# Two-layer hybrid encoder step on one core: order at the ends of FFN-in, the pool windows, the gates, the row products and the sample transposes

## The reference

```python
def _swiglu(u, w_in, w_out):
    h = u @ w_in                        # 1024 -> 2 x 2816
    a, b = h[..., :D_FF], h[..., D_FF:]
    return (jax.nn.silu(a) * b) @ w_out
# layer 0's mixer: means over the last 2, 4, 8, 16 rows per group of 256 channels,
# minus the row itself, times a 256x256 matrix per group
# layer 1's mixer (mLSTM): p = u @ w_in gives q, k, v, o and 2 x 4 gates; chunked scan over
# tokens with running maxima m of the gate sums; h = num / max(|den|, exp(-m)); norm; gate by o
for i in range(DEPTH):
    x = x + 0.5 * _swiglu(_rmsnorm(x, norm_ffn1[i]), ffn1_w_in[i], ffn1_w_out[i])
    x = x + mixer_i(_rmsnorm(x, norm_mix[i]))
    x = x + 0.5 * _swiglu(_rmsnorm(x, norm_ffn2[i]), ffn2_w_in[i], ffn2_w_out[i])
return _rmsnorm(x, norm_final), states
```

## Time and profile before

| what | value |
|---|---|
| median of 3 runs | 1940.64 us (1940.33 to 1942.73) |
| profiled execution, its own time | 1941.61 us |
| its span in the trace | 1939.8 us |
| PE busy | 1889.8 us (97%) |
| DVE busy | 1265.5 us (65%) |
| ACT busy | 861.1 us (44%) |
| POOL busy | 348.7 us (18%) |
| mean granted TensorE clock | 0.989 |

### The profile page before, as it was taken

One profiled execution on the slowest core, in us unless ns is written; L12 is line 12 of the kernel. 1 busy time (PEld: TensorE's weight loads), 2 busy tenths in 40 slices (PEclk: granted clock), 3 DMA queues, 4 the chain that ended last, 5 costly groups with the idle time before them and its releaser, 6 DMA issues.

```text
span 1939.8 us, 34552 instructions
## 1 busy us (share of the span) xinstructions
PE 1889.8 (97%) x13912; PEld 1865.1 (96%) x13912; DVE 1265.5 (65%) x1999; ACT 861.1 (44%) x1503; POOL 348.7 (18%) x365
## 2 busy tenths in 40 slices
PE   7999999998999999999999999999999999999996
PEld 6999999998999999999999999999989999999996
DVE  6884487657884488678853886452546987448742
ACT  6552355346553255445532553222434465235521
POOL 2220122121220121132201221200002522012122
PEclk8999999999999999999999999999999999999998
DMA  6763577323764476438644763321113476357531
GB/s 182 163 152 104 118 168 151 104 70 71 168 147 110 117 165 143 109 93 183 135 130 106 169 135 96 93 96 56 55 44 110 103 174 156 91 131 163 124 90 64
DMA packets 115854, 234.70 MB, mean 121 GB/s; under 512 B 13233, under 2 KB 13249, under 8 KB 115697
## 3 DMA queue, kind: packets, MB, share of 16 engines
q1 hardware_dynamic: 76464, 160.59, 27.7%
q0 software_dynamic: 38208, 69.42, 21.8%
q10 hardware_dynamic: 1024, 2.49, 0.4%
HBM read 228.92 MB, written 3.53 MB: 120 GB/s over the span
## 4 chain that ended last, share of the span: by engine, by line
PE 85%; DVE 5%; DMA 4%; issue 4%; ACT 2%; POOL 0%; DVEq 0%; ACTq 0%; POOLq 0%
PE ps L1688 43%; PE ps L1678 39%; DVE w_lo L1140 2%; DMA raw_z<-in_ffn_in 1%; DMA raw_y<-in_ffn_in 1%; ACT w_hi L712 1%; DMA w_raw<-in_ffn_out 1%; PE ps L1992 0%; DMA x<-in_x 0%; PE ps L1995 0%; PE ps L1982 0%; DVE tmp L1259 0%; DMA raw_a<-in_ffn_in 0%; DVE rstd L1211 0%; DVE raw_z L1146 0%
## 5 line engine op out<-in xcount | busy, mean ns | idle before, releaser
L1688 PE MATMUL ps<-u,w_hi 128*128 128x288 f32 x4928 | 994.7, 298 | 29.7 <-DVE w_lo L1140 11.0
L1688 PEld LDWEIGHTS ps<-u,w_hi 128*128 128x128 f32 x4928 | 796.7, 189 | 36.4 <-DVE w_lo L1140 19.4
L1688 PE MATMUL ps<-u,w_lo 128*128 128x288 f32 x2464 | 731.0, 297 | 0.0
L1688 PEld LDWEIGHTS ps<-u,w_lo 128*128 128x128 f32 x2464 | 465.6, 189 | 0.0
L1678 PE MATMUL ps<-h_hi,w_lo 128*128 128x288 f32 x1408 | 302.8, 296 | 0.0
L1678 PE MATMUL ps<-h_hi,w_hi 128*128 128x288 f32 x1408 | 302.7, 296 | 0.0
L1678 PE MATMUL ps<-h_lo,w_hi 128*128 128x288 f32 x1408 | 302.5, 296 | 0.0
L712 ACT ACTIVATE w_hi<-w_raw 128x768 fp32r<-128x768 f32 (+3 forms) x164 | 137.1, 837 | 341.4 <-PE ps L1678 305.1
L1140 DVE TENSOR_TENSOR w_lo<-w_raw,w_hi 128x768 fp32r<-128x768 f32 (+3 forms) x164 | 170.4, 1039 | 175.2 <-ACT w_hi L712 172.6
L574 POOL DMA_DIRECT2D raw_y<-in_ffn_in x88 | 75.8, 864 | 864.0 <-DVE raw_z L1146 847.8
L1678 PEld LDWEIGHTS ps<-h_lo,w_hi 128*128 128x128 f32 x1408 | 226.6, 189 | 0.0
(11 more groups left out here) (246 smaller groups left out, 2179.0 us busy)
## 6 DMA issues: line engine op xcount, KB each, us to landing
raw_a<-in_ffn_in SPq DMA_DIRECT2D x132, 256.0 KB, 4.2
w_raw<-in_ffn_out SPq DMA_DIRECT2D x64, 384.0 KB, 3.1
raw_y<-in_ffn_in SPq DMA_DIRECT2D x88, 256.0 KB, 3.6
raw_x<-in_ffn_in SPq DMA_DIRECT2D x88, 256.0 KB, 2.7
raw_x<-in_ffn_in POOLq DMA_DIRECT2D x88, 256.0 KB, 6.1
raw_y<-in_ffn_in POOLq DMA_DIRECT2D x88, 256.0 KB, 5.0
raw_z<-in_ffn_in POOLq DMA_DIRECT2D x88, 256.0 KB, 4.7
w_raw<-in_ffn_out SPq DMA_DIRECT2D x64, 320.0 KB, 2.9
```

The costliest lines, as they stand in the source:

```text
L1688: mm = pe.matmul(dst, w, m, start=prod in ("M1", "M2", "M5") and kp == 0 and p == 0, stop=kp == KP - 1 and p == 2, skip_group_check=prod i ...
```

## The change

It has six parts, each with its place in the diff.

1. Ends of FFN-in, DVE. After M6(10), M2(10), M3(9), M3(10) and M4(10) DVE no longer calls `ahead`; after `h_mul(10)` it makes up for it. The splits of the first two units of FFN-out thus move behind `up_two(10)`, those of the next two behind `h_mul(10)`.
2. Ends of FFN-in, ACT. `silu(10)` goes ahead of `h_high(9)`, both go ahead of the copies that `ahead` makes at M3(10) and M4(10).
3. At the mLSTM's norm `ahead(U_M)` goes ahead of `root` on ACT and of `rstd_of` on DVE. It splits one unit, the fourth projection's weights, which take the entries of the gates' weights.
4. Gates. PE does the first two steps of the first projection between the gates' seventh and eighth step, and the norm's mean comes behind the projection's third step.
5. Row products. "cols" and "mb"(0) move from behind the first v projection to the third and the sixth step of the second one.
6. Pool windows: the 15 columns of the next chunk join the product of 128 columns (143 in one), so five products a tile in place of eight. The fp32 products for the sample (L1957, L1968, L2020) become transposes, 8, 4 and 8 of them.

```diff
@@ scalar, ffn_in
-                    ahead(u)
+                    if (prod, n) == ("M4", PAIRS - 1):
+                        silu(f, ph, PAIRS - 1)
+                        h_high(f, ph, PAIRS - 2)
+                    if (prod, n) != ("M3", PAIRS - 1):
+                        ahead(u)
...
-                h_high(f, ph, PAIRS - 2)
-                silu(f, ph, PAIRS - 1)
                 h_high(f, ph, PAIRS - 1)
@@ scalar, before the mLSTM
+            ahead(U_M)
             root(N_MIX)
             act.dma_start(c_st[1][:, :, :], a["state_c"]).then_inc(state_landed, 16)
-            ahead(U_M)
@@ vector, ffn_in
-                    ahead(u)
+                    if (prod, n) != ("M3", PAIRS - 2) and (n < PAIRS - 1 or prod in ("M1", "M5", "M7")):
+                        ahead(u)
                 h_mul(f, ph, PAIRS - 1)
+                ahead(f.unit(ph, "M4", PAIRS - 1))
                 h_low(f, ph, PAIRS - 1)
@@ tensor, pool_windows
-                    pe.matmul(ps[:, window_bank(g) + m, HIST:CH], zs[0], bands[:, g, IN + HIST:NEXT], start=True, stop=True)
+                    pe.matmul(ps[:, bank, HIST:CH + HIST], zs[0], bands[:, g, IN + HIST:START],
+                              start=False, stop=True, skip_group_check=True)
                     for c in range(1, NB - 1):
-                        pe.matmul(ps[:, window_bank(g) + m, c * CH:(c + 1) * CH], zs[c], bands[:, g, IN:NEXT],
-                                  start=True, stop=False)
-                        mm = pe.matmul(ps[:, window_bank(g) + m, c * CH:c * CH + HIST], zs[c - 1], bands[:, g, NEXT:START],
-                                       start=False, stop=True)
+                        end = min(SEQ, (c + 1) * CH + HIST)
+                        mm = pe.matmul(ps[:, bank, c * CH:end], zs[c], bands[:, g, IN:IN + end - c * CH],
+                                       start=False, stop=True, skip_group_check=True)
@@ tensor, gates and first projection
+            for k in range(DT - 1):
+                gates_mm(k)
+            pe.wait_ge(lo_split, U_M + 2)
+            for k in range(DT):
+                if k == 2:
+                    gates_mm(DT - 1).then_inc(unit_used, 1)
+                elif k == 3:
+                    norm(N_MIX)
+                mm = block_mm(U_M + 1, k, u_tile(k), 2, k == 0, k == DT - 1)
             mm.then_inc(unit_used, 1)
-            norm(N_MIX)
-            pe.wait_ge(x_ready, 5 * DT)
-            for g in range(1, 9):
+            for g in range(2, 9):
@@ tensor, items
-                    mm = pe.matmul(ps[0:DEC_SEQ, b + 1, 0:P], og[:, n, SEQ:TOK], ident[:, :],
-                                   start=True, stop=True)
+                    mm = pe.transpose(ps[0:DEC_SEQ, b + 1, 0:P], og[:, n, SEQ:TOK], ident[:, :])
@@ tensor, v projections
-                project(U_M + 9 + t, 2 * ((9 + t) % 2))
+                inside = {2: lambda: item("cols", 0, 0), 5: lambda: item("mb", 0, 1)} if t == 1 else {}
+                project(U_M + 9 + t, 2 * ((9 + t) % 2), inside)
                 for k, (kind, n) in enumerate(AFTER_V[t], ITEM_AT[t]):
-                    item(kind, n, k)
+                    if t:
+                        item(kind, n, k)
@@ tensor, heads_back
-                pe.matmul(ps[:, b + 1, 0:DEC_SEQ], v_one[0:DEC_SEQ, NB - 1, h, d0:d0 + P],
-                          ident[0:DEC_SEQ, 0:DEC_SEQ], start=True, stop=True).then_inc(y_psum, 1)
+                pe.transpose(ps[:, b + 1, 0:DEC_SEQ], v_one[0:DEC_SEQ, NB - 1, h, d0:d0 + P],
+                             ident[0:DEC_SEQ, 0:DEC_SEQ]).then_inc(y_psum, 1)
```

More of the change, by code:

```diff
@@ L1798, in u_tile, with project @@
                 return um_hi[:, k, :], um_lo[:, k, :]
-            def project(n, bank, middle=None, middle_at=3, each=None):
+            def project(n, bank, inside={}, each=None):
                 pe.wait_ge(lo_split, n + 1)
@@ L1808, in project @@
                         mm.then_inc(each, 1)
-                    if k == middle_at and middle:
-                        middle()
+                    if k in inside:
+                        inside[k]()
             def norm_cols(n):
@@ L1879, in pool_windows @@
                     zs = [z[:, g, c, m * P:(m + 1) * P] for c in range(NB - 1)]
-                    pe.matmul(ps[:, window_bank(g) + m, 0:HIST], zs[0], bands[:, g, START:LAST], start=True, stop=True)
-                    pe.matmul(ps[:, window_bank(g) + m, HIST:CH], zs[0], bands[:, g, IN + HIST:NEXT], start=True, stop=True)
+                    bank = window_bank(g) + m
+                    pe.matmul(ps[:, bank, 0:HIST], zs[0], bands[:, g, START:LAST], start=True, stop=True)
+                    pe.matmul(ps[:, bank, HIST:CH + HIST], zs[0], bands[:, g, IN + HIST:START],
+                              start=False, stop=True, skip_group_check=True)
                     for c in range(1, NB - 1):
-                        pe.matmul(ps[:, window_bank(g) + m, c * CH:(c + 1) * CH], zs[c], bands[:, g, IN:NEXT],
-                                  start=True, stop=False)
-                        mm = pe.matmul(ps[:, window_bank(g) + m, c * CH:c * CH + HIST], zs[c - 1], bands[:, g, NEXT:START],
-                                       start=False, stop=True)
+                        end = min(SEQ, (c + 1) * CH + HIST)
+                        mm = pe.matmul(ps[:, bank, c * CH:end], zs[c], bands[:, g, IN:IN + end - c * CH],
+                                       start=False, stop=True, skip_group_check=True)
                     mm.then_inc(pool_psum, 1)
@@ L1915, in _, with gates_mm @@
             pe.wait_ge(x_ready, 5 * DT - 1)
-            for k in range(DT):
+            def gates_mm(k):
                 pe.wait_ge(u_ready, DT + k + 1)
@@ L1921, in _ @@
                                        u[:, h * HALF:(h + 1) * HALF], start=k + p == 0,
-                                       stop=k + p == DT)
+                                       stop=k + p == DT, skip_group_check=True)
+                return mm
+            for k in range(DT - 1):
[7 more added lines that the diff above has]
+                mm = block_mm(U_M + 1, k, u_tile(k), 2, k == 0, k == DT - 1)
             mm.then_inc(unit_used, 1)
-            norm(N_MIX)
-            pe.wait_ge(x_ready, 5 * DT)
-            for g in range(1, 9):
+            for g in range(2, 9):
                 if g > 2:
@@ L1964, in item @@
                                   start=True, stop=True)
-                        if L == P:
-                            mm = pe.transpose(ps[:, b + 1, h * P:(h + 1) * P], k_c, ident[:, :])
-                        else:
-                            mm = pe.matmul(ps[0:L, b + 1, h * P:(h + 1) * P], k_c, ident[:, :],
-                                           start=True, stop=True)
+                        mm = pe.transpose(ps[0:L, b + 1, h * P:(h + 1) * P], k_c, ident[:, :])
                 mm.then_inc(core_psum, 1)
@@ L2031, in _ @@
                     middle, behind = IN_O[j]
-                    project(U_M + 17 + j, 2 * ((17 + j) % 2), middle=lambda: in_o(middle))
+                    project(U_M + 17 + j, 2 * ((17 + j) % 2), {3: lambda: in_o(middle)})
                     in_o(behind)
                 else:
-                    project(U_M + 17 + j, 2 * ((17 + j) % 2), middle=first_heads, middle_at=DT - 2)
+                    project(U_M + 17 + j, 2 * ((17 + j) % 2), {DT - 2: first_heads})
             pe.wait_ge(proj_read, 26)
```

## The result

The changed kernel takes 1933.34 us (median of 6 runs) where the kernel before, on the same chip, takes 1941.68 us; the ratio is 0.9942 with a 95% interval of 0.9925 to 0.9958. Two of its six executions were slow, 3057.7 us at a mean granted clock of 0.55 and 4606.3 us at 1.00, for a reason that no run here shows; the ratio leaves them out, and the median of the other four is 1931.5 us. A second measurement on another occasion gave 0.9948 (0.9928 to 0.9968). It is faster by 0.5 to 0.6%, where 0.47% was forecast, and both medians lie in the forecast range. The profiled execution took 1928.8 us with a span of 1927.0, and that of before 1941.61 with 1939.8.

The account below looks back on a forecast made before the run. PE was taken as the bound, busy 1889.8 of 1939.8 us. Terms 3.0 + 0.6 + 1.0 + 0.9 + 3.6 = 9.1 us, from the median of 1940.64, gave 1931.5 us, 0.47% faster; range 1927.0 to 1937.0.

Parts of the forecast that it names:

- Ends of FFN-in, 3.0 us: At M4(10) in four of eight stages, PE's waits of 0.33, 1.17, 0.18 and 1.35 us behind `up_two` all go.
- The step on ACT: At the ends of FFN-in, `silu(10)` ahead of `h_high(9)` on ACT only shortens `h_mul(10)`'s wait; no gain of its own.
- the slack of 0.6 us: At step 11 of FFN-out's first output tile, `h_low(10)` ends near 358.0 us and PE wants it at 358.6.
- the slower rival: DVE bounds FFN-in's end: moved splits wait for copies, `h_low(10)` 2.5 us late in eight stages; 1951 us, chance 0.05.
- Pool windows, 0.6 us: In the pool stage each tile saves 0.31 us; DVE's chain moves up by two tiles' worth; ends 0 and 2.5.
- Gates, 1.0 us: Two projection steps fill 1.6 us of the 1.68 us wait; a 0.5 us wait for DVE's read comes before the third projection.
- Row products, 0.9 us: Behind the 4-row products among the v projections, fewer clock falls; between 3.4 us won and 1.7 us lost.
- Half a fall: For the row products, taken between both 1.7 us falls to 1.2 GHz going and a third coming; 0.9 us.
- Transposes, 3.6 us: Sample's fp32 products as transposes: 0.20 us saved for each of 16, 0.1 for each of 4 in "sk".
- the lower bound: For the transposes, 1.5 us, if a pause now lies before the transpose's successor.
- The page's rule: Transposes do not count as busy for the clock gate; by it, 3.6 us less one or two falls.

Follow-up runs that it names:

- the transposes' own experiment: The kernel before with only the decode sample's fp32 products against the identity turned into transposes; ratio 0.9984 (0.9972 to 0.9997).
- The parts measured alone: The kernel before with one part each: ends of FFN-in (ratio 0.9971), pool windows (0.9987), the sample's transposes (0.9984), row products (1.0010).

## Why the prediction was right, step by step

The sum was 9.1 us; the median of 1931.5 us lies 10.2 below that of before, and the ratios give 11.3 (8.2 to 14.6) and 10.1 us. The direction and the places were right, but most terms were off, in both directions. Ends and windows were 2.0 us too low, the gates, the row products and the transposes 2.2 us too high, so that the sum fits this well is in part luck.

- **Ends of FFN-in, 3.0 us:** right for the profile it was read from, and low as a mean: the old order's pauses at M4(10) are 2.4 to 5.8 us over five executions, and with the other short pauses the ends are worth about 4.1. The step on ACT was wrong. "Only shortens `h_mul(10)`'s wait" is false: with ScalarE's old order the slack of 0.6 us is used up, and about 5 us stand at step 11. The mechanism of the slower rival was real; what kept it away is the half of the edit that I had costed at nothing. The rival asked whether the copies for the splits are late, and it is `h_high(9)` behind a copy that waits for a transfer.
- **Pool windows, 0.6 us:** the term was mis-sized, about 1.5 us by itself. I took 0.31 us for a full product and scaled it by 143/128. But 0.31 is the price of one that stands behind a product of 15 columns; behind another wide one it is 0.24, in the kernel before (431.20 to 431.44 us) as in the 143-column row after. The tile saves 0.55 us and not 0.31, twice on the path, and 0.3 us more comes from z(3).
- **Gates, 1.0 us:** 0.5. The order of copy, table load, root and read came as worked out, and PE reached the third projection within 0.2 us of where I had it, but the read of q ended 0.5 us later: the copy began 0.9 us behind the start of the gates' last step where I had 0.6, from reciprocal to read it took 9.2 us and not 9.1, and the rest is rounding. A pause of 0.5 became one of 1.14.
- **Row products, 0.9 us:** -0.3. Half a fall was a guess between two cases, and neither came: the falls stay, one to five of them, and the switches cost 0.3. What was missed is that their number changes with the execution of one and the same program.
- **Transposes, 3.6 us:** 3.1 by the ratio. The single prices were wrong in both directions: 0.43 us for each of the eight in "vt" where I took 0.20, a loss of 0.15 for each of the four in "sk" where I took a gain of 0.1, and 0.16 in `heads_back` (the step is 0.20 us, it was 0.36); a pause of 0.76 us came back at "sk"(3), the kind named for the lower bound.
- **The page's rule.** The Trainium skill, TensorE: Matmul & The Clock Gate, Part 4: PE-mode transpose, says that transposes do not count as busy for the clock gate in the way other products do; by that the clock could fall where they replace products. Among the items the measurement decides against it: 1.00 over their stretch in the transposes' own experiment and in every other profile with them. In `heads_back` it stays open, as the fall there came with and without them.

The parts measured alone give -0.29, -0.13, -0.16 and +0.10%, together -0.48%; the whole is -0.58 and -0.52%, and the gates account for about 0.03% by the profile. Each of these has an interval of 0.12 to 0.2% to either side, so they agree, but they could not show a difference of 2 us.

## What to carry to other kernels

When two engines' orders are changed together, cost each one without the other: here VectorE's new order without ScalarE's is 9 us slower than both together. An engine that copies what a transfer brings should have no short step that another engine needs queued behind that copy. And products with few rows can cost more than their time: piled up, as in the kernel before (4.25 and 2.1 us) and the changed one (3.2 and 2.1 us), they were followed by one to five falls in each of eleven profiles; in pieces of 0.9 to 1.5 us with 2.5 us or more of full products between, by none in three, for 0.3 to 0.4 us a piece. A transpose in place of a small product has to be priced in its own place: the same edit won 0.43 us in one and lost 0.15 in another.

## What the runs showed that I had not expected

The scatter of the kernel before (1937 to 1949 us) has two visible sources. One is the clock: 1.7 us for each fall to 1.2 GHz, behind 4-row products and behind pauses (in the changed kernel at 453 us behind one of 4.41 us, at 1525 behind one of 2.38), from one to five falls in one place for nearly the same products. The other is transfers that land up to 2.5 us later, for copies at the ends of stages. Both are larger than most single edits here, and one profile shows one draw of them. Why a stretch gets one fall in one execution and five in another stays open; no run here varied the start of the program in time.
